# Turning the probabilities of the 18 short attention pairs on VectorE instead of TensorE

## The reference, cut to what matters

```python
p = masked_softmax(jnp.einsum('btgrd,btkgd->bgrtk', qb, kg) * scale, ok)
return jnp.einsum('bgrtk,btkgd->btgrd', p.astype(v.dtype), vg)
```

## Time and profile before

| | |
|---|---|
| median of three runs | 2998.04 us |
| profiled execution | 2996.23 us, span 2994.4 us |
| TensorE busy | 2983.7 us, 100% |
| VectorE busy | 1977.1 us, 66% |
| ScalarE busy | 1531.6 us, 51% |
| GpSimd busy | 296.5 us, 10% |
| DMA | 55.6% of 16 engines, 185 GB/s |

### The profile page before, as it was taken

One profiled execution on the slowest core, in us unless ns is written; L12 is line 12 of the kernel. 1 busy time (PEld: TensorE's weight loads), 2 busy tenths in 40 slices (PEclk: granted clock), 3 DMA queues, 4 the chain that ended last, 5 costly groups with the idle time before them and its releaser, 6 DMA issues.

```text
span 2994.4 us, 36986 instructions
## 1 busy us (share of the span) xinstructions
PE 2983.7 (100%) x13949; PEld 2496.3 (83%) x13949; DVE 1977.1 (66%) x2605; ACT 1531.6 (51%) x2098; POOL 296.5 (10%) x245
## 2 busy tenths in 40 slices
PE   9999999999999999999999999999999999999999
PEld 7888888988888888888888888888888888888887
DVE  6666667789578676666666655568876666666554
ACT  6656555555654664543444444467845444444443
POOL 0043200145000450000000000001000000000000
PEclk9999999999999999999999999999999999999999
DMA  9664345555445544556555555565455566555554
GB/s 344 216 223 156 127 131 183 173 182 175 141 157 195 183 151 145 185 195 196 192 188 186 194 205 188 191 199 181 142 197 189 191 195 196 190 185 194 202 192 145
DMA packets 256565, 553.92 MB, mean 185 GB/s; under 512 B 9809, under 2 KB 42721, under 8 KB 245697
## 3 DMA queue, kind: packets, MB, share of 16 engines
q1 hardware_dynamic: 255616, 550.82, 55.6%
q0 software_dynamic: 544, 1.48, 0.2%
q10 hardware_dynamic: 288, 0.07, 0.0%
HBM read 550.24 MB, written 2.10 MB: 184 GB/s over the span
## 4 chain that ended last, share of the span: by engine, by line
PE 98%; DVE 1%; ACT 0%; DMA 0%; issue 0%; ACTq 0%
PE psum L749 42%; PE psum L2491 32%; PE psum L2632 16%; PE psum L2768 2%; PE psum L1593 2%; PE psum L1609 1%; PE psum L1621 1%; PE psum L1582 1%; PE psum L2230 0%; PE psum L978 0%; DVE weights_lo L558 0%; PE psum L1821 0%; PE psum L2101 0%; PE psum L1596 0%; DMA shape_consts<-in_consts 0%; PE psum L1869 0%
## 5 line engine op out<-in xcount | busy, mean ns | idle before, releaser
L558 DVE TENSOR_TENSOR weights_lo<-weights,weights_hi 128x1024 fp32r<-128x1024 f32 (+2 forms) x1015 | 1261.5, 1252 | 720.7 <-ACT weights_hi L540 717.7
L540 ACT ACTIVATE weights_hi<-weights 128x1024 fp32r<-128x1024 f32 (+2 forms) x1015 | 1055.2, 1048 | 1257.1 <-PE psum L749 534.9
L749 PE MATMUL psum<-weights_hi,act_hi 128*128 128x512 f32 (+3 forms) x1952 | 763.3, 391 | 0.3 <-DVE weights_lo L558 0.2
L749 PE MATMUL psum<-weights_hi,act_lo 128*128 128x512 f32 (+3 forms) x1952 | 749.5, 384 | 0.0
L749 PE MATMUL psum<-weights_lo,act_hi 128*128 128x512 f32 (+3 forms) x1952 | 748.8, 384 | 0.0
L2491 PE MATMUL psum<-weights_hi,act_hi 128*128 128x512 f32 x1408 | 548.3, 389 | 0.0
L2491 PE MATMUL psum<-weights_hi,act_lo 128*128 128x512 f32 x1408 | 548.1, 389 | 0.0
L2491 PE MATMUL psum<-weights_lo,act_hi 128*128 128x512 f32 x1408 | 548.1, 389 | 0.0
L749 PEld LDWEIGHTS psum<-weights_hi,act_hi 128*128 128x128 f32 x1952 | 367.1, 188 | 69.7 <-issue 4.9
L749 PEld LDWEIGHTS psum<-weights_hi,act_lo 128*128 128x128 f32 x1952 | 366.7, 188 | 67.7
L749 PEld LDWEIGHTS psum<-weights_lo,act_hi 128*128 128x128 f32 x1952 | 367.4, 188 | 63.4
(11 more groups left out here) (253 smaller groups left out, 1956.8 us busy)
## 6 DMA issues: line engine op xcount, KB each, us to landing
weights<-in_ffn_w_gate SPq DMA_DIRECT2D x88, 1024.0 KB, 5.2
weights<-in_ffn_w_up SPq DMA_DIRECT2D x88, 1024.0 KB, 5.2
weights<-in_ffn_w_down SPq DMA_DIRECT2D x88, 1024.0 KB, 4.8
weights<-in_odd_w_in SPq DMA_DIRECT2D x40, 1024.0 KB, 5.1
weights<-in_even_w_in SPq DMA_DIRECT2D x36, 1024.0 KB, 5.1
weights<-in_w_out SPq DMA_DIRECT2D x32, 1024.0 KB, 5.0
weights<-in_rnn_w_in SPq DMA_DIRECT2D x32, 1024.0 KB, 5.6
weights<-in_attn_w_qkv SPq DMA_DIRECT2D x24, 1024.0 KB, 5.1
```

The costliest lines, as they stand in the source:

```text
L540: e.nc.scalar.activation(e.WH[(2 * slot + b) % HL][:, 0:n // 2], e.RAW[slot][:, b * n // 2:(b + 1) * n // 2], ACT.Copy).then_inc(self.hi.s ...
L558: e.nc.vector.tensor_tensor(e.WL[s][:, 0:n // 2], e.RAW[slot][:, b * n // 2:(b + 1) * n // 2], e.WH[s][:, 0:n // 2].bitcast(F32), ALU.subt ...
L749: last = e.nc.tensor.matmul(e.PS[:, banks.start + m, 0:w], a, x, start=(kk == 0 and n == 0), stop=(kk == KT - 1 and n == 2))
```

## The change

For the 18 short pairs TensorE no longer turns the probabilities, and ScalarE no longer copies them from PSUM. VectorE turns them with 16 transposes of 32 partitions x 64 elements (a 32x32 block of both products at once), from `E` straight into a new buffer `PTS` in SBUF. This happens at VectorE step `slot+2`, behind the clamp and reciprocal of the pair before, and so one step earlier than the copy was. VectorE waits there for the pair's own two exponentials, for the value products of the short pair before (they read `PTS`), and ahead of the last transpose for the copy of the pair before, which keeps the count of `pcopied` in order. The long pairs and the memory pairs are as before. An exponential behind a short pair waits for VectorE's transposes and no longer for TensorE's.

```diff
+    def flips(self, n):
+        return self.pturned.sem, self.pturned.at(n - len([k for k in self.short if k < n]))
+
+    def flip(self, dve, n):
+        older = [k for k in self.short if k < n]
+        dve.wait_ge(self.exp.sem, self.exp.at(2 * n + 2))
+        if older:
+            dve.wait_ge(self.pv.sem, self.pv.at(older[-1] + 1))
+        for r in range(4):
+            for c in range(4):
+                if n and r + c == 6:
+                    dve.wait_ge(self.pcopied.sem, self.pcopied.at(n))
+                ins = self.e.nc.vector.transpose(self.PTS[32 * c:32 * c + 32, :, 32 * r:32 * r + 32], self.E[32 * r:32 * r + 32, :, 32 * c:32 * c + 32])
+        ins.then_inc(self.pcopied.sem, 1)
...
     def tensor(self, pe, s):
...
-                    last = nc.tensor.matmul(self.O(n)[:, i, :], self.PT[:, i, kt * P:(kt + 1) * P], p["v"][i][:, kt, :], start=(kt == 0),
+                    turned = self.PTS if n in self.short else self.PT
+                    last = nc.tensor.matmul(self.O(n)[:, i, :], turned[:, i, kt * P:(kt + 1) * P], p["v"][i][:, kt, :], start=(kt == 0),
...
-        if s - self.TURN in self.at:
+        if s - self.TURN in self.at and self.at[s - self.TURN] not in self.short:
...
     def scalar(self, act, s):
...
-            if n:
-
-                act.wait_ge(self.pturned.sem, self.pturned.at(n))
+            if n - 1 in self.short:
+
+                act.wait_ge(self.pcopied.sem, self.pcopied.at(n))
+            elif n:
+
+                act.wait_ge(*self.flips(n))
...
-        if s - 2 - self.TURN in self.at:
+        if s - 2 - self.TURN in self.at and self.at[s - 2 - self.TURN] not in self.short:
...
     def vector(self, dve, s):
...
+        if s - 2 in self.at and self.at[s - 2] in self.short:
+            self.flip(dve, self.at[s - 2])
```

More of the change, by code:

```diff
@@ L1505, with __init__ @@
     TURN, VALUES, STATS = 1, 2, 304
-    def __init__(self, e, turns, pairs, E, PT):
+    def __init__(self, e, turns, pairs, E, PT, short=None):
         self.e, self.turns, self.pairs, self.E, self.PT = e, turns, pairs, E, PT
@@ L1515, in __init__ @@
         self.sums = [n for n, p in enumerate(pairs) if p["sum"] == "pair"]
+        self.short = [n for n, p in enumerate(pairs) if short is not None and p["keys"] == P]
+        self.PTS = short
     def end(self):
@@ L1521, in end @@
             s.advance(k)
-        for s in (e.s_score, e.s_negmax, e.s_clamped, e.s_inverse, e.s_pturned, e.s_pcopied, e.s_pv, e.s_stored):
+        e.s_pturned.advance(n - len(self.short))
+        for s in (e.s_score, e.s_negmax, e.s_clamped, e.s_inverse, e.s_pcopied, e.s_pv, e.s_stored):
             s.advance(n)
@@ L1634, in scalar @@
                                      accum_out=self.col(1, n)[:, i:i + 1]).then_inc(self.exp.sem, 1)
-        if s - 2 - self.TURN in self.at:
+        if s - 2 - self.TURN in self.at and self.at[s - 2 - self.TURN] not in self.short:
             n = self.at[s - 2 - self.TURN]
-            act.wait_ge(self.pturned.sem, self.pturned.at(n + 1))
+            act.wait_ge(*self.flips(n + 1))
             self.copy(act, n)
@@ L1752, in __init__ @@
         buffers = pr[:, :, c["kc"]:c["kc"] + 512].rearrange("p j (i k) -> p j i k", i=2)
-        super().__init__(e, turns, pairs, buffers[:, 0], buffers[:, 1])
+        super().__init__(e, turns, pairs, buffers[:, 0], buffers[:, 1], pr[:, 0, c["mz"]:c["mz"] + T].rearrange("p (i k) -> p i k", i=2))
         late = EVEN_CHUNKS[10][0]
@@ L2059, in __init__ @@
         buffers = pr[:, :, c["iq"]:c["iq"] + 512].rearrange("p j (i k) -> p j i k", i=2)
-        super().__init__(e, turns, pairs, buffers[:, 0], buffers[:, 1])
+        super().__init__(e, turns, pairs, buffers[:, 0], buffers[:, 1], pr[:, 0, c["iq"] + 512:c["iq"] + 512 + T].rearrange("p (i k) -> p i k", i=2))
         self.roped = self.heads.final(c["ik"])
```

## The result

The changed kernel takes 3005.88 us (median of 7 runs, 3004.61 to 3007.97), the kernel before beside it 2997.66 us (7 runs). The ratio is 1.0028, with a 95% interval of 1.0019 to 1.0038. The prediction was 2999.4 us with a range up to 3005.0: it missed. The profiled execution took 3004.61 us with a span of 3002.8 us, 8.4 us more than before.

The account below looks back on a forecast made before the run. TensorE, almost never waiting, was taken as the bound. Lateness of +2.7 us after the even layer's waits and gains, less 1.35 in the odd layer, gave +1.35 us: 2997.6 profiled, 2999.4 on the median; range 2994.5 to 3005.

Parts of the forecast that it names:

- the last rival: Behind the wait near 412 us, a granule at 1.2 in place of 2.4 GHz takes some 5.5 us more: 3005; chance 0.04.
- place 3: Pairs 44 and 45 share `PTS`, five row transposes follow in VectorE's step 47; TensorE waits 3.4 us for scores of 47.
- Behind it nothing comes back: After pairs 44 and 45: later granules have their weights converted, VectorE catches up in memory pairs; lateness stays +2.7 us.
- the ledger: Running count of how much later (+) or earlier (-) TensorE stands than before, through the kernel.
- A transpose costs TensorE 0.11 us: 36 transposes at L1621, priced by spacing of starts: 0.225 us for a short pair, 4.05 us saved in all.
- The rival that took the whole duration: Each L1621 transpose is worth 0.273 us, 9.8 us in all; with the waits -3.5 us, 2994.5; chance 0.06.
- Place 1: First pair: TensorE's L1858 in step 25 waits for scaled compressed probabilities behind the new transposes; +0.8 us, pair's gain included.
- Slots 26 to 38: Seven pairs gain 1.6 us; VectorE's lateness just fits 5 us of cover, so 0 taken, 0 to +1 kept.
- a wait in the alternating slots: Sign of being wrong: TensorE waits showing in the alternating slots, where none was forecast.
- Places 2 and 3: Pairs 40 and 41, then 44 and 45, share one `PTS`; TensorE waits 0.95 us, then 3.4 us, for scores.
- The odd layer: Six strictly alternating short pairs, `PTS` always free, VectorE has 25 us left; all six gains stay, -1.35 us.
- One rival: All covered: waits don't reach TensorE because transposes overlap or cost 0.16 us; without any wait -4.05 us, 2994.0; chance 0.18.

Follow-up runs that it names:

- two buffers: Changed kernel with a second `PTS` in the even layer, used in turn: 2996.48 us against 2997.24 for the kernel before, ratio 0.9997.
- the odd layer's gap: Kernel before, with a wait for pair 38's value products and 26 constant transposes added in the odd layer's VectorE step 41: 3004.03 us, ratio 1.0023.
- the copied kernel: Changed kernel with each short pair's 16 transposes replaced by one copy of the unturned probabilities: 2993.78 us, ratio 0.9986 to the kernel before.
- 17 pairs against 18: Changed kernel, second even-layer `PTS`, first pair's transposes behind the compressed scaling; 17 leaves slot 34 on TensorE: 2994.80 us; 18: 2995.23 us.
- The first of these kernels: Changed kernel with the next stage's row transposes begun at step 48, not 47: 3001.79 us, ratio 1.0016 to the kernel before.

## Why the prediction was wrong

**The step that failed** is the last rival, "The gap at place 3 costs TensorE its clock", with a chance of 0.04, and with it "Behind it nothing comes back" in the ledger. It happened, at about the price given (5.5 us forecast for it, 4.5 measured), and the time of that case, 3005, is near what came out. That is partly luck: 2999.4 + 4.5 are 3003.9, and the rest came from other terms that were sized too low. The forecast had the gap right (3.4 us against 3.66), and stopped there. The reason that I gave against it, a clock of 1.00 in the first 20 us, doesn't bear on it: there TensorE began late and then ran, while at place 3 it stopped in the middle of dense work. The kernel before has no such stop at all, so nothing in its trace could speak against the rival; 0.04 was far too sure. The experiments show the cause in both directions: the gap alone, put into the kernel before, costs 8.1 us, and the change without that gap (two buffers) costs nothing that can be measured.

The Trainium skill, "TensorE: Matmul & The Clock Gate", Part 1, "HAM oscillation — how this bites in real kernels", prices an idle gap inside a matmul kernel by the time spent throttled behind it, of which half is lost. By that page of the Trainium skill the 10.4 us would cost an estimated 5.2, and the 6.8 us of the odd layer's gap 3.4; the traces have 4.5 and the runs 1.7, so here the rule is an upper end.

**Point by point.**
- A transpose costs TensorE 0.11 us, not 0.27: right in the mechanism and a little high (0.10 from the copied kernel; by the ledger the fourteen pairs with no wait beside them gave 0.90 + 0.54 + 1.15 = 2.59 us, 0.185 a pair in place of 0.225). The rival that took the whole duration is out.
- 0.24 us for a transpose of 32x64 on VectorE: right, 236 ns, 3.98 us for sixteen against 3.84.
- Place 1: 1.10 us waited, ledger +1.22 of which 0.18 was there before; +0.8 forecast.
- Slots 26 to 38 at 0: off by 0.73 us, inside the 0 to +1 kept, but a wait in the alternating slots was one of the signs named for being wrong. Slot 36's scores need the exponentials of pair 35. Its maximum, at 324.87 us before, came at 330.98, 6.1 us later, which is more than the five microseconds of cover. The transposes of pair 34 stand ahead of it (3.97 us), and turning that pair on TensorE took this wait away (17 pairs against 18).
- Places 2 and 3: 1.12 and 3.66 us against 0.95 and 3.4, by the chains as written.
- The odd layer: -1.15 in the ledger against -1.35; the runs with it alone give -1.4.
- The sum: +1.35 forecast, +8.4 measured. Of the 7.05 between them 4.5 is the clock, 0.73 the stretch, 0.42 place 1 and the start, 0.26 and 0.17 places 3 and 2, 0.20 the odd layer. Of the 0.8 left, 0.36 is that the eight pairs between place 1 and slot 42 gave 0.18 us each and not 0.225, and 0.16 is what slot 36's scores lost beyond their wait; 0.25 is not assigned.
- One rival was a little off in its own sum: with transposes of 0.16 us place 3 would keep 3.4 - 16 x 0.08 = 2.1 us, not 1.9. Nothing hangs on it.

**What stays open.** Gaps of 3.37 to 4.71 us lowered the clock in each of the four kernels that had one, and none of their 32 runs had a mean clock of 1.000. Gaps of 1.3 to 1.4 us did so in one of the three profiled: 1.42 us at 415.60 lowered it, 1.37 us at 416.49 and 1.33 us at 808.76 didn't. The first of these kernels also had the waits of places 1 and 2 and of slot 36, the last 30 us earlier, and the turns on VectorE; the other two had none of it. No experiment separates what TensorE did before the gap from where the gap lay, and I don't settle it.

## What to carry to other kernels

When the bound engine is TensorE and it never waits, ask of a change what is the longest gap it opens, not only what the gaps add up to: here a gap of 3.7 us cost 8. A buffer shared by two successors turns a wait that was idle time into time on the path as soon as the work behind it grows from 0.3 to 4 us, so give it a second buffer before moving work there. And a stall's cost can be measured alone, by putting the stall into the old kernel.

## What the runs showed of the hardware

**The clock falls without any wait, too.** In six of the thirteen profiled executions, of kernels with and without the change, TensorE ran at half clock near 211 us, far ahead of any edit. There it has just done 32 matmuls of 15 columns; the next ones of 416 columns start 0.35 us apart in place of 0.19, until 214 us (TensorE's timeline with two buffers, then the window):

```profile
207.03 3.66 PE L1882 MATMUL psum<-cmp_k_t,proj 128*128 128x15 f32 x32
...
211.37 0.55 PE L749 MATMUL psum<-weights_hi,act_lo 128*128 128x416 f32 x1
211.72 0.55 PE L749 MATMUL psum<-weights_hi,act_hi 128*128 128x416 f32 x1
...
214.44 0.35 PE L749 MATMUL psum<-weights_hi,act_hi 128*128 128x416 f32 x1
214.62 0.35 PE L749 MATMUL psum<-weights_lo,act_hi 128*128 128x416 f32 x1
...
210.00:214.00 4.00, 4.00 (x17) 3.85 (x17) 1.41 (x6) 0.50 (x2) 0.42 (x2) 0.57 1.02 345
```

The executions of before and after that the ledger compares have 1.00 in this window, so it is no part of the 8.4 us. The scatter between runs of one kernel goes with the clock. The runs of the kernel before in the first batch, grouped by mean granted clock, took 2996.44 us at 1.000 (16 runs), 2998.13 at 0.999 (13) and 3000.69 at 0.998 (4); the second and third batch repeat the first two within 0.3 us. That is why two of the comparisons above are also given between runs of equal mean clock.

**Some small operations of VectorE are slow beside GpSimd, the transposes aren't.** Ahead of pair 34's transposes, while GpSimd works without a pause (timelines of the changed kernel, VectorE then GpSimd):

```profile
323.45 1.24 DVE L1709 TENSOR_SCALAR stats<-stats 128x2 f32<-128x2 f32 x1
324.93 0.99 DVE L1714 TENSOR_TENSOR stats<-stats,proj 128x2 f32<-128x2 f32 x1
325.84 3.97 DVE L1573 STREAM_TRANSPOSE proj<-proj 32x64 f32<-32x64 f32 x16
...
322.52 2.15 POOL L1402 TENSOR_TENSOR rotation_temps<-proj,shape_consts 128x512 f32<-128x512 f32 x1
324.62 1.27 POOL L1402 TENSOR_TENSOR proj<-proj,shape_consts 128x512 f32<-128x512 f32 x1
```

The first is the operation that takes 0.16 us in the earlier trace rows, eight times longer. The 288 transposes lie between 225 and 243 ns wherever they stand. The Trainium skill, "GPSIMD Engine Reference", Key points, names VectorE instructions in a 2-port mode or with two SBUF inputs as those that contend; the transposes agree with it, and so does the second operation, with two inputs. Whether the first ran in a 2-port mode no row shows. The kernel before has the same slow operation in the same stretch (VectorE's timeline):

```profile
320.04 1.26 DVE L1683 TENSOR_SCALAR stats<-stats 128x2 f32<-128x2 f32 x1
```

So it is part of what fills VectorE there, before as after, and no delay that the change brought. How much of the 0.73 us of the stretch it makes was not tested.
